# A sink as a score column, weight remainders and residual scaling on GpSimd, and first weights in pieces, in a four-layer transformer kernel

## The chip, the cores and the metric

The kernel runs on one core of one Trainium2 chip. A core has TensorE (PE) for matrix products, VectorE (DVE), ScalarE (ACT), GpSimd (POOL) and SyncE (SP), which here only issues DMAs. The engines run their own instruction streams and meet at semaphores. The metric is the device time of one launch in microseconds (us), lower is better.

## What is computed

Two blocks of two layers each, on 512 tokens of width 1024. Layers 0 and 1 hold full attention and a chunked state-space mixer. Layers 2 and 3 hold attention in a band of 128 tokens with a sink, and differential attention. The four layers end with a gated feed-forward part. The change touches the beginning and layers 2 and 3, of which this is the core:

```python
def windowed_gqa_sink(q, k, v, sink):          # 8 query heads, 2 key heads, blocks of 128
    scores = einsum(q, k) * D ** -0.5          # each block of queries sees up to 3 blocks of keys
    scores = where(|kpos - qpos| <= 128, scores, NEG)
    m = maximum(max(scores), sink)             # one number per head
    p = exp(scores - m)
    p = p / (sum(p) + exp(sink - m))
    return einsum(p, v)

def diff_attention(q, k, v, lam):              # 4 heads, two score maps each
    p = softmax(einsum(q, k) * Dk ** -0.5)
    return einsum(p[:, :, 0] - lam * p[:, :, 1], v)
```

The first block ends with `rms_norm(x, final_norm_w)`, so that the residual which enters layer 2 has to be multiplied by that weight and by the reciprocal root of its mean square ("residual scaling").

## The kernel before

**Exact products from rounded ones.** An f32 operand is split into hi (rounded by ACT, as `fp32r`) and lo (the remainder f32 - hi, formed by DVE). A product is three matmuls, hi*hi, hi*lo and lo*hi (`three`, lines 1568 to 1570, which all large products share).

**Weights.** They come in groups g of 128 x 2048 (1 MB), 190 in all, through two sets of buffers by the parity of g: `w_raw` (DMA), `w_hi` (ACT, `split_hi`, line 321), `w_lo` (DVE, `split_lo`, line 771). PE waits for `w_ready`, which w_lo raises (`enter`). SP loads group g once w_lo of g - 2 is done. `split_hi(g)` waits until PE is through with group g - 2.

**Start.** SP issues the parameters, group 0, the eight tiles of x (128 x 512), group 1, the constants. ACT makes w_hi of group 0, then for each tile h_mix_hi and its square, then w_hi of group 1. DVE makes w_lo of group 0, eight h_mix_lo (`norm_lo`, line 777), then w_lo of group 1. GpSimd sums the squares (line 1495). PE makes the projection of the two groups for four blocks of tokens t: all t over k = 0 to 3 of group 0, then over k = 4 to 7 of group 1. Within the second it sums the squares by matmuls with a column of ones (`stats`, line 1632); from it come var (DVE, line 788) and rstd (GpSimd, line 1503), by which evictions scale.

**Layers 2 and 3.** They take 9 groups of projections, counted from g0, then four of w_out. While PE is at groups g0 + 3 to g0 + 8, DVE rotates heads (`rope_b(n, t)`: n = 0 queries of the band, 1 and 2 queries and keys of the differential part, t = block), for which GpSimd raises variances to -1/2 (line 1545).

**Banded attention** has 16 steps i of a block and a head pair (i = 4t + j), software-pipelined by hand. In one round PE makes scores of step i (line 1671) and adds masks by bf16 matmuls with an identity (line 1679), turns the probabilities of step i - 2 (line 1703) and multiplies those of i - 3 with v (line 1727). DVE takes maxima of the two heads' scores (line 1373), the minimum with the negated sink (line 1377), copies half of the turned probabilities (line 905). ACT makes the exps (line 408) and the other half (line 416). Scores alternate between two pairs of PSUM banks: scores of i wait for exps of i - 2. Between the rounds PE also turns the eight tiles of the differential q and k (`turn`, line 1654) through one bank, each waiting for hi (ACT, line 400) and lo (DVE, line 888) of the tile before. Once in a block the softmax factors are made (DVE line 1391, PE line 1714), applied (line 911) and split (lines 426 and 917).

Into the same rounds, in program order, are put w_hi and w_lo of two groups of w_out (rounds 12 and 14), and in layer 2 the eight residual scalings on DVE (line 1411, rounds 7 to 14).

**Differential attention** follows with 16 steps of its own: maxima (line 1423), exps (line 730), a combination of the two maps (line 1435), transposes (line 2107), products (line 2121).

## Time and profile before

| | us |
|---|---|
| median of 3 runs | 2510.55 (2508.02 to 2511.35) |
| the profiled execution, its own time | 2512.78 |
| its span, first to last instruction | 2510.6 |
| PE busy | 2430.3 (97%) |
| DVE busy | 1474.9 (59%) |
| ACT busy | 944.8 (38%) |
| GpSimd busy | 210.5 (8%) |

The profile is one execution. Busy time of PE says little by itself, since matmuls overlap and their ends are modelled; the distance between the starts of consecutive matmuls tells more: 0.23 us for 512 columns when PE runs at its higher clock. Waits are read from the timeline, where a row carries in square brackets how long its engine had been idle before it and which instruction released it.

### The profile page before, as it was taken

The page shows a single profiled execution, that of the slowest core. Times are in us where ns is not written, and L with a number is a line of the kernel's source. Part 1 is how long each engine was busy: PE and PEld are TensorE (multiplying, and loading weights), DVE is VectorE, ACT ScalarE, POOL GpSimd, SP SyncE. Part 2 cuts the span into 40 slices and gives each one's busy share as a digit, 9 for nine tenths or more (in the row PEclk, how much of TensorE's full clock was granted, in tenths as well). Part 3 has the DMA queues.
Part 4 walks back from the last instruction along what each step waited for, and adds up shares of the span by engine and source line. Part 5 has one row for each costly group of instructions (what it writes and reads, how often), then busy time and mean ns, then how long its engine had stood idle before and what let it go on. Part 6 is the DMA issues. An engine that isn't in the chain of part 4 may idle for free.

```text
span 2510.6 us, 30919 instructions
## 1 busy us (share of the span) xinstructions
PE 2430.3 (97%) x12468; PEld 1989.0 (79%) x12468; DVE 1474.9 (59%) x2074; ACT 944.8 (38%) x1496; POOL 210.5 (8%) x143
## 2 busy tenths in 40 slices
PE   7999999999999999999999799999999989999999
PEld 6767888888876788888887578888888767888887
DVE  5867543435586754343567766545466776655554
ACT  4465322213446432222444563222243465322222
POOL 2001200000200110000132011000012101100000
PEclk9999999999999999999999899999999999999999
DMA  4200222222311032222321002222232110222222
GB/s 172 78 35 1 101 96 89 101 101 101 102 68 35 1 103 99 101 95 90 118 84 68 35 9 102 94 100 101 91 111 99 53 35 25 94 101 101 100 85 101
DMA packets 30238, 205.32 MB, mean 82 GB/s; under 512 B 3344, under 2 KB 3472, under 8 KB 6288
## 3 DMA queue, kind: packets, MB, share of 16 engines
q1 hardware_dynamic: 30096, 203.35, 22.8%
q8 instruction: 99, 1.62, 0.3%
q14 instruction: 43, 0.35, 0.0%
HBM read 201.24 MB, written 2.10 MB: 81 GB/s over the span
## 4 chain that ended last, share of the span: by engine, by line
PE 85%; DVE 8%; DVEq 3%; ACT 2%; issue 1%; ACTq 0%; DMA 0%; POOL 0%; SPq 0%
PE bank L1568 25%; PE bank L1570 25%; PE bank L1569 25%; PE bank L1727 1%; PE bank L1671 1%; PE bank L1703 1%; PE bank L1953 1%; PE bank L1901 1%; PE bank L1714 1%; PE bank L1654 1%; DVE w_lo L771 1%; DVE b_p L1435 1%; DVE neg_max L1423 1%; ACT w_hi L321 1%; DVEq L1430 1%
## 5 line engine op out<-in xcount | busy, mean ns | idle before, releaser
L771 DVE TENSOR_TENSOR w_lo<-w_raw,w_hi 128x2048 fp32r<-128x2048 f32 (+1 forms) x190 | 434.0, 2284 | 404.9 <-ACT w_hi L321 404.4
L1568 PE MATMUL bank<-h_ffn_hi,w_hi 128*128 128x512 f32 x1408 | 548.6, 390 | 0.0
L1570 PE MATMUL bank<-h_ffn_hi,w_lo 128*128 128x512 f32 x1408 | 547.8, 389 | 0.0
L1569 PE MATMUL bank<-h_ffn_lo,w_hi 128*128 128x512 f32 x1408 | 547.7, 389 | 0.0
L321 ACT ACTIVATE w_hi<-w_raw 128x2048 fp32r<-128x2048 f32 (+1 forms) x190 | 360.1, 1895 | 473.0 <-PE bank L1570 424.5
L1570 PEld LDWEIGHTS bank<-h_ffn_hi,w_lo 128*128 128x128 f32 x1408 | 264.3, 188 | 55.1
L1569 PEld LDWEIGHTS bank<-h_ffn_lo,w_hi 128*128 128x128 f32 x1408 | 264.3, 188 | 54.7
L1568 PEld LDWEIGHTS bank<-h_ffn_hi,w_hi 128*128 128x128 f32 x1408 | 264.3, 188 | 54.5
L1568 PE MATMUL bank<-act_hi,w_hi 128*128 128x512 f32 x704 | 273.9, 389 | 0.0
L1569 PE MATMUL bank<-act_lo,w_hi 128*128 128x512 f32 x704 | 273.9, 389 | 0.0
L1570 PE MATMUL bank<-act_hi,w_lo 128*128 128x512 f32 x704 | 273.9, 389 | 0.0
L1568 PE MATMUL bank<-w_hi,h_mix_hi 128*128 128x512 f32 (+2 forms) x512 | 191.0, 373 | 20.1 <-DVE h_mix_lo L777 13.5
L442 ACT ACTIVATE act_hi<-up 128x512 fp32r<-128x512 f32 x88 | 55.7, 633 | 371.0 <-DVE up L950 371.0
L1495 POOL TENSOR_TENSOR sq_sum<-sq_sum,sq 128x512 f32<-128x512 f32 x56 | 95.5, 1706 | 1180.7 <-ACT sq L339 1178.6
L1569 PE MATMUL bank<-w_lo,h_mix_hi 128*128 128x512 f32 (+2 forms) x512 | 187.8, 367 | 0.0
L1570 PE MATMUL bank<-w_hi,h_mix_lo 128*128 128x512 f32 (+2 forms) x512 | 187.7, 367 | 0.0
L947 DVE TENSOR_TENSOR up<-bank,rstd_bc 128x512 f32<-128x512 f32 x88 | 60.9, 692 | 193.9 <-PE bank L1570 193.9
L1569 PEld LDWEIGHTS bank<-act_lo,w_hi 128*128 128x128 f32 x704 | 132.1, 188 | 27.5
L1570 PEld LDWEIGHTS bank<-act_hi,w_lo 128*128 128x128 f32 x704 | 132.1, 188 | 27.5
L1568 PEld LDWEIGHTS bank<-act_hi,w_hi 128*128 128x128 f32 x704 | 132.1, 188 | 27.3
L929 DVE TENSOR_TENSOR gate<-bank,rstd_bc 128x512 f32<-128x512 f32 x88 | 60.8, 691 | 117.6 <-PE bank L1570 115.9
L1568 PEld LDWEIGHTS bank<-w_hi,h_mix_hi 128*128 128x128 f32 x512 | 97.3, 190 | 39.1 <-issue 14.3
(305 smaller groups left out, 3396.3 us busy)
## 6 DMA issues: line engine op xcount, KB each, us to landing
w_raw<-weights SPq DMA_DIRECT2D x186, 1024.0 KB, 4.7
w_raw<-weights SPq DMA_DIRECT2D x4, 544.0 KB, 3.7
residual<-x_in SPq DMA_DIRECT2D x8, 256.0 KB, 5.8
x_out<-residual SPq DMA_DIRECT2D x8, 256.0 KB, 2.0
cst<-consts SPq DMA_DIRECT2D x1, 960.0 KB, 10.2
par_b<-params_b SPq DMA_DIRECT2D x1, 627.0 KB, 11.2
par_a<-params_a SPq DMA_DIRECT2D x1, 244.0 KB, 2.7
```

The source lines that it names most:

```text
L321: nc.scalar.activation(w_hi[s][:, cols], w_raw[s][:, cols], ACT.Copy).then_inc(w_hi_done, 1)
L442: act.activation(act_hi[:, 2 * i + j, :], up[j][:, :], ACT.Identity).then_inc(act_hi_done, 1)
L771: nc.vector.tensor_tensor(w_lo[s][:, cols], w_raw[s][:, cols], w_hi[s][:, cols].bitcast(F32), ALU.subtract).then_inc(w_ready, 1)
L929: nc.vector.tensor_tensor(gate[j][:, 1:SEQ + 1], bank[src][:, :], rstd_bc[:, :], ALU.mult).then_inc(bank_free[src], 1)
L947: nc.vector.tensor_tensor(up[j][:, :], bank[src][:, :], rstd_bc[:, :], ALU.mult).then_inc(bank_free[src], 1)
L1423: nc.vector.tensor_reduce(neg_max[:, n:n + 1], bank[DS_BANKS[i % 2][c]][:, :], AX.X, ALU.max, negate=True).then_inc(dmax_done, 1)
L1430: dve.drain()
L1435: nc.vector.scalar_tensor_tensor(p1, p2, tiny[:, i:i + 1], p1, ALU.mult, ALU.add).then_inc(dw_done, 1)
L1495: nc.gpsimd.tensor_tensor(sq_sum[:, :], sq_sum[:, :], sq[k % 2][:, :], ALU.add).then_inc(sum_done, 1)
L1568: mm(out, ahi, bhi, start=start, stop=False)
L1569: mm(out, ahi, blo, start=False, stop=False)
L1570: return mm(out, alo, bhi, start=False, stop=stop)
```

## The change

1. *Sink.* TensorE writes the sink as one more column behind the scores of each head: a product of 64 rows of the sink value with one column of the identity. Maximum and exp run over that column too, so that the minimum with the negated sink, the separate exps and their sum into the denominator go. Each maximum releases its own exp.
2. *Remainders and residual in layers 2 and 3.* w_lo of groups g0 + 9 and g0 + 10 goes to GpSimd, in four pieces of 512 columns each, with the residual scaling as two products a tile. ACT makes their w_hi in halves, in rounds 4, 5, 8 and 9. DVE waits for both before it uses the residual.
3. *Start.* Groups 0 and 1 come in four pieces each, alternating with the tiles of x. PE goes through k outside and t inside.
4. *Smaller moves.* In layers 2 and 3 `split_hi(g0 + 2)` stands ahead of the wait for rstd, and `split_lo(g0 + 4)` after the second rope and not the fourth. The differential maximum runs over both banks in one instruction.

```diff
             for k in range(KT):
+                cols = first_cols(k)
+                sp.dma_start(w_raw[k // 4][:, cols], weights[k // 4][:, cols]).then_inc(first_in[k], 16)
                 sp.dma_start(residual[:, k, :], x_in[:, k, :]).then_inc(x_arrived[k], 16)
-            sp.dma_start(w_raw[1][:, :], weights[1]).then_inc(w_in[1], 16)
...
+                cols = slice(part * GW // 2, (part + 1) * GW // 2)
+                nc.scalar.activation(w_hi[s][:, cols], w_raw[s][:, cols], ACT.Copy)
+                if part == 1:
+                    act.drain().then_inc(w_hi_done, 1)
...
-            split_hi(0)
             for k in range(KT):
+                cols = first_cols(k)
+                act.wait_ge(first_in[k], 16)
+                nc.scalar.activation(w_hi[k // 4][:, cols], w_raw[k // 4][:, cols], ACT.Copy).then_inc(w_hi_done if k % 4 == 3 else first_hi, 1)
                 wait_tile(-1, 24 + k)
                 norm_hi(h_mix_hi, k, mix_weight(0, k))
-                norm_square(0, k)
-            split_hi(1)
+                if k >= 1:
+                    norm_square(0, k - 1)
+            norm_square(0, KT - 1)
...
+                split_hi(g0 + 2)
                 act.wait_ge(rstd_ready, 2 * lay + 1)
-                split_hi(g0 + 2)
...
                 for i in range(20):
-                    if i >= 4 and i % 4 == 0 and i < 17:
-                        sink_exp(i // 4 - 1)
-                    if i in (12, 14):
-                        split_hi(g0 + 3 + i // 2)
+                    if i in (4, 5, 8, 9):
+                        split_half(g0 + IN_B + i // 8, i % 2)
...
                     if i < 16:
-                        pair_exp(lay, i, 0, window(i // 4)[1] * P, probs)
+                        pair_exp(lay, i, 0, window(i // 4)[1] * P + 1, probs)
...
                 for t in range(TB):
                     rope_b(0, t)
-                split_lo(g0 + 4)
+                    if t == 1:
+                        split_lo(g0 + 4)
...
-                        nc.vector.tensor_reduce(neg_max[:, c:c + 1], bank[S_BANKS[i % 2][par_]][:, 0:window(i // 4)[1] * P],
-                                                AX.X, ALU.max, negate=True)
-                    dve.drain()
-                    j = i % 4
-                    nc.vector.tensor_tensor(neg_max[:, 2 * i:2 * i + 2], neg_max[:, 2 * i:2 * i + 2], neg_sink[:, 2 * j:2 * j + 2],
-                                            ALU.min).then_inc(max_done, 2)
+                        nc.vector.tensor_reduce(neg_max[:, c:c + 1], bank[S_BANKS[i % 2][par_]][:, 0:window(i // 4)[1] * P + 1],
+                                                AX.X, ALU.max, negate=True).then_inc(max_done, 1)
...
-                    dve.wait_ge(sink_out, 4 * l + t + 1)
                     dve.wait_ge(e_done, base + 8 * t + 8)
-                    nc.vector.tensor_tensor(denom[:, c], denom[:, c], tiny[:, c], ALU.add)
-                    dve.drain()
                     nc.vector.reciprocal(recip[:, c], denom[:, c]).then_inc(recip_ready, 1)
...
-                    if i in (12, 14):
-                        split_lo(g0 + 3 + i // 2)
-                    if l == 0 and 7 <= i < 7 + KT:
-                        k = i - 7
-                        nc.vector.scalar_tensor_tensor(residual[:, k, :], residual[:, k, :], par_a[:, 0, A_FIN + k:A_FIN + k + 1],
-                                                       rstd_bc[:, :], ALU.mult, ALU.mult)
...
-                    for c in range(2):
-                        n = 2 * i + c
-                        dve.wait_ge(ds_done, 32 * l + n + 1)
-                        nc.vector.tensor_reduce(neg_max[:, n:n + 1], bank[DS_BANKS[i % 2][c]][:, :],
-                                                AX.X, ALU.max, negate=True).then_inc(dmax_done, 1)
+                    dve.wait_ge(ds_done, 32 * l + 2 * i + 2)
+                    nc.vector.tensor_reduce(neg_max[:, 2 * i:2 * i + 2], both_banks(DS_BANKS[i % 2], 512),
+                                            AX.X, ALU.max, negate=True).then_inc(dmax_done, 2)
...
+                    for n in range(4):
+                        cols = slice(n * GW // 4, (n + 1) * GW // 4)
+                        nc.gpsimd.tensor_tensor(w_lo[s][:, cols], w_raw[s][:, cols], w_hi[s][:, cols].bitcast(F32), ALU.subtract)
+                    pool.drain().then_inc(w_ready, 1)
...
+                split_lo(g0 + IN_B)
+                if l == 0:
+                    pool.wait_ge(bc_ready, broadcasts(2 * lay) + 1)
+                    for k in range(KT):
+                        x = residual[:, k, :]
+                        nc.gpsimd.tensor_tensor(x, x, par_a[:, 0, A_FIN + k:A_FIN + k + 1].to_broadcast([P, SEQ]), ALU.mult)
+                        pool.drain()
+                        if k == 3:
+                            split_lo(g0 + IN_B + 1)
+                        nc.gpsimd.tensor_tensor(x, x, rstd_bc[:, :], ALU.mult)
+                    pool.drain().then_inc(x_scaled, 1)
+                else:
+                    split_lo(g0 + IN_B + 1)
...
+                for k in range(KT):
+                    s, kk = divmod(k, 4)
+                    if kk == 3:
+                        pe.wait_ge(w_ready, s + 1)
+                    else:
+                        pe.wait_ge(first_ready, 3 * s + kk + 1)
+                    pe.wait_ge(h_ready, k + 1)
+                    if k == KT - 1:
+                        pe.wait_ge(consts_ready, 1)
+                        stats(0)
+                    for t in range(TB):
...
                 if masked:
+                    for par_ in range(2):
+                        rows = slice(par_ * HD, (par_ + 1) * HD)
+                        head = B_SINK + 2 * j + par_
+                        mm(bank[S_BANKS[i % 2][par_]][:, nb * P:nb * P + 1], par_b[rows, lay - LAYERS, head:head + 1].to_broadcast([HD, P]),
+                           ident[rows, par_ * HD:par_ * HD + 1], start=False, stop=False)
```

**ACT at the start of the program.** Before:

```order
L321 ACT_TABLE_LOAD [waits w_in0]
L321 ACTIVATE w_hi<-w_raw 128x2048 [waits par_in]
L332 ACTIVATE h_mix_hi<-residual,par_a 128x512 [waits x_arrived0]
L339 ACTIVATE sq_sum<-residual 128x512
L332 ACTIVATE h_mix_hi<-residual,par_a 128x512 [waits x_arrived1]
```

And now:

```order
L491 ACT_TABLE_LOAD [waits first_in0]
L491 ACTIVATE w_hi<-w_raw 128x512 [waits par_in]
L350 ACTIVATE h_mix_hi<-residual,par_a 128x512 [waits x_arrived0]
L491 ACTIVATE w_hi<-w_raw 128x512 [waits first_in1]
L350 ACTIVATE h_mix_hi<-residual,par_a 128x512 [waits x_arrived1]
L357 ACTIVATE sq_sum<-residual 128x512
```

The first tile of h_mix_hi stands behind a quarter of a group and not a whole one, and a square comes one tile later.

**DVE in round 12 of the banded attention of layer 2** (the exps of the second to last block; L771 is w_lo, L1411 the residual scaling). Before:

```order
L1373 TENSOR_REDUCE neg_max<-bank 128x1 [waits s_done] x2
L1377 TENSOR_TENSOR neg_max<-neg_max,neg_sink 128x2
L888 TENSOR_TENSOR b_kt_lo<-bank,b_kt_hi 128x512 [waits t_hi_done]
L905 COPY b_pt<-bank 128x384 [waits o_done,pt_done]
L771 TENSOR_TENSOR w_lo<-w_raw,w_hi 128x2048 [waits w_hi_done]
L1411 SCALAR_TENSOR_TENSOR residual<-residual,par_a,rstd_bc 128x512
L917 TENSOR_TENSOR b_ot_lo<-b_on,b_ot_hi 128x4x128 [waits o_hi_done]
L1389 TENSOR_TENSOR denom<-denom,tiny 128x8 [waits e_done,sink_out]
L1391 RECIPROCAL recip<-denom 128x8
```

And now:

```order
L1393 TENSOR_REDUCE neg_max<-bank 128x1 [waits s_done] x2
L903 TENSOR_TENSOR b_kt_lo<-bank,b_kt_hi 128x512 [waits t_hi_done]
L920 COPY b_pt<-bank 128x384 [waits o_done,pt_done]
L932 TENSOR_TENSOR b_ot_lo<-b_on,b_ot_hi 128x4x128 [waits o_hi_done]
L1400 RECIPROCAL recip<-denom 128x8 [waits e_done]
```

The minimum, w_lo, the scaling and the sum with the sink's exp are gone from DVE's row.

**GpSimd in layer 2**, from the last powers for the ropes (head_rs) on. Before:

```order
L1549 TENSOR_TENSOR head_rs<-ssq,neg_half 128x4x2 [waits hvar_ready]
L1545 TENSOR_TENSOR head_rs<-ssq,neg_half 128x8 [waits hvar_ready] x8
L1554 TENSOR_TENSOR head_rs<-ssq,neg_half 128x4 [waits gn_var] x4
L1495 TENSOR_TENSOR sq_sum<-sq_sum,sq 128x512 [waits sq_done] x7
L1503 TENSOR_TENSOR rstd<-var,neg_half 128x4 [waits var_ready]
```

And now:

```order
L1546 TENSOR_TENSOR head_rs<-ssq,neg_half 128x8 [waits hvar_ready] x8
L1560 TENSOR_TENSOR w_lo<-w_raw,w_hi 128x512 [waits w_hi_done,w_ready]
L1560 TENSOR_TENSOR w_lo<-w_raw,w_hi 128x512 x3
L1569 TENSOR_TENSOR residual<-residual,par_a 128x512 [waits bc_ready]
L1573 TENSOR_TENSOR residual<-residual,rstd_bc 128x512
...
L1569 TENSOR_TENSOR residual<-residual,par_a 128x512
L1560 TENSOR_TENSOR w_lo<-w_raw,w_hi 128x512 [waits w_hi_done,w_ready]
L1560 TENSOR_TENSOR w_lo<-w_raw,w_hi 128x512 x3
L1573 TENSOR_TENSOR residual<-residual,rstd_bc 128x512
```

The first remainder and, behind it, the two products for each tile have come to GpSimd; the second remainder stands between the two products of tile 3.

## Rows read from the trace of the kernel before

**Rows 1.** Page part 4, shares of the chain that ended last, by engine.

```profile
PE 85%; DVE 8%; DVEq 3%; ACT 2%; issue 1%; ACTq 0%; DMA 0%; POOL 0%; SPq 0%
```

**Rows 2.** Timeline, start: start us, us, engine, line, operation, count [idle before <-releaser].

```profile
6.04 1.28 ACT L321 ACT_TABLE_LOAD   x1 [6.04 <-DMA w_raw<-weights]
...
7.33 1.91 ACT L321 ACTIVATE w_hi<-w_raw 128x2048 fp32r<-128x2048 f32 x1
...
9.35 2.29 DVE L771 TENSOR_TENSOR w_lo<-w_raw,w_hi 128x2048 fp32r<-128x2048 f32 x1 [8.35 <-ACT w_hi L321]
...
13.55 0.77 PE L1568 MATMUL bank<-w_hi,h_mix_hi 128*128 128x512 f32 x1 [13.55 <-DVE h_mix_lo L777]
```

**Rows 3.** Windows: length, PE, PEld, DVE, ACT, POOL (count), granted clock, DMA, GB/s.

```profile
13.50:19.60 6.10, 5.99 (x12) 3.41 (x13) 6.10 (x4) 4.62 (x8) 5.62 (x4) 1.00 0.81 338
19.60:33.20 13.60, 13.60 (x61) 11.25 (x60) 9.42 (x25) 2.44 (x2) 3.10 (x2) 1.00 0.12 41
1312.40:1317.00 4.60, 4.53 (x13) 3.59 (x14) 4.28 (x10) 0.00 (x0) 1.64 (x1) 0.63 0.64 228
1373.80:1433.80 60.00, 48.24 (x474) 36.72 (x474) 42.38 (x97) 34.96 (x101) 0.00 (x0) 0.89 0.10 36
1996.70:2054.20 57.50, 47.61 (x462) 36.31 (x462) 36.08 (x86) 33.78 (x97) 0.00 (x0) 0.88 0.11 38
1433.80:1480.00 46.20, 39.23 (x283) 29.75 (x281) 41.03 (x90) 35.55 (x105) 3.03 (x3) 0.96 0.00 1
```

**Rows 4.** Timeline, from stats to w_lo of the third group of layer 0.

```profile
33.45 0.94 PE L1632 MATMUL bank<-ones,sq_sum 128*128 128x1 f32 x8
...
35.73 1.11 ACT L321 ACTIVATE w_hi<-w_raw 128x1088 fp32r<-128x1088 f32 x1 [13.66 <-POOL rstd L1503]
...
36.88 1.29 DVE L771 TENSOR_TENSOR w_lo<-w_raw,w_hi 128x1088 fp32r<-128x1088 f32 x1 [2.28 <-ACT w_hi L321]
```

**Rows 5.** Timeline, PE's waits for w_lo in layers 2 and 3.

```profile
1286.55 0.39 PE L1568 MATMUL bank<-w_hi,h_mix_hi 128*128 128x256 f32 x1 [1.31 <-DVE w_lo L771]
...
1312.47 0.50 PE L1568 MATMUL bank<-w_hi,h_mix_hi 128*128 128x512 f32 x1 [2.34 <-DVE w_lo L771]
...
1935.64 0.50 PE L1568 MATMUL bank<-w_hi,h_mix_hi 128*128 128x512 f32 x1 [2.83 <-DVE w_lo L771]
```

**Rows 6.** Timeline, end of layer 0: sums of squares on GpSimd beside DVE.

```profile
617.46 2.26 POOL L1495 TENSOR_TENSOR sq_sum<-sq_sum,sq 128x512 f32<-128x512 f32 x1 [331.43 <-ACT sq L339]
...
618.49 1.79 DVE L777 SCALAR_TENSOR_TENSOR h_mix_lo<-residual,par_a,h_mix_hi 128x512 fp32r<-128x512 f32 x1
...
622.28 1.34 POOL L1495 TENSOR_TENSOR sq_sum<-sq_sum,sq 128x512 f32<-128x512 f32 x1 [2.56 <-ACT sq L339]
...
622.43 0.69 DVE L794 TENSOR_TENSOR residual<-bank,residual 128x512 f32<-128x512 f32 x1
```

**Rows 7.** Chain in order of time, rounds 5 and 6 of layer 2: start, us, what.

```profile
1387.06 1.02 PE bank L1714 x16
...
1388.52 0.72 PE bank L1671 x6
```

**Rows 8.** Groups by line and form, DVE, band of layer 2: busy us, mean ns.

```profile
L1373 DVE TENSOR_REDUCE neg_max<-bank 128x1 f32<-128x384 f32 x16 | 8.1, 549 | 4.8 <-PE bank L1679 4.8
L1411 DVE SCALAR_TENSOR_TENSOR residual<-residual,par_a,rstd_bc 128x512 f32<-128x512 f32 x8 | 5.9, 744 | 0.0
...
L771 DVE TENSOR_TENSOR w_lo<-w_raw,w_hi 128x2048 fp32r<-128x2048 f32 x2 | 4.6, 2282 | 0.0
...
L1377 DVE TENSOR_TENSOR neg_max<-neg_max,neg_sink 128x2 f32<-128x2 f32 x15 | 2.4, 160 | 1.1
```

**Rows 9.** Timeline, two waits of PE in the band of layer 2.

```profile
1412.98 0.39 PE L1671 MATMUL bank<-b_kd_hi,h_mix_hi 64*128 64x256 f32 x2 [1.52 <-DVE b_kt_lo L888]
...
1417.26 1.98 PE L1714 MATMUL bank<-cst,recip 128*64 128x128 f32 x16 [2.78 <-DVE recip L1391]
```

**Rows 10.** Groups by line and form, DVE, differential attention of layer 2.

```profile
L1423 DVE TENSOR_REDUCE neg_max<-bank 128x1 f32<-128x512 f32 x32 | 20.6, 685 | 1.2 <-PE bank L2097 0.8
```

76 lines of the change are left out of this document (47 added, 29 removed).

## The prediction

> **What bounds the kernel now.** I read the chain on the page first: PE carries 85% of it [rows 1]. So another engine matters only where PE waits for it. The second view was who PE waits for, the third the timeline and windows around those waits, whose rows stand here. The largest is 13.5 us before the first matmul [rows 2]; later ones name DVE (w_lo, b_kt_lo, recip) [rows 5, 9]. The reader should see two costs at each: the idle time, and the matmuls behind it at twice the pitch. The twelve matmuls from 13.5 on fill 6.1 us, against 61 in the next 13.6 us (0.22 each); at 1312.4 to 1317 the granted clock is 0.63, between the levels 1.2 and 2.4 GHz [rows 3].
>
> **Start.** Before, w_hi (1.91) and w_lo (2.29) of a whole group precede the first operand of PE, and PE begins at 13.55, released by the first h_mix_lo [rows 2]. Now each k brings 512 columns. A w_hi piece costs about 0.63 (an estimate from 1.91 for 2048 and 1.11 for 1088 columns [rows 2, 4]), a w_lo piece 0.69 in the same way from 2.29 and 1.29. The whole megabyte had landed by 6.04 [rows 2]; the three quarters that are no longer waited for are 0.79 MB, 2.3 us at the 338 GB/s of the next stretch [rows 3], so the first quarter lands near 3.8, with the par_a in front of it and the shorter run-up say 4.1. Then table load 1.28, w_hi to 6.05, h_mix_hi to 6.7, w_lo to 6.75, h_mix_lo to 7.5: PE starts at 7.5, not 13.55. The new order gives 12 matmuls per k, 5.2 us at the slow pitch and 2.72 at the fast. ACT needs 1.7 per k; DVE and GpSimd, which exclude each other here (below), about 2.6. PE is therefore the bound from k = 1 on. The first pair ends at 7.5 + 96 x 0.227 + 0.8 (stats) + 2.4 (slow phase, 9 to 14 matmuls at 0.2 extra) = 32.5, against 39.8 before (stats at 33.45, 0.8 for them, then 24 x 0.227, and 0.1 [rows 4]): 7.3 gained. But stats now stand 12 matmuls before that end and not 24. From the end of stats to w_lo of group 2 it takes 3.85 us (rstd, w_hi, w_lo [rows 4]); 2.72 of it is covered, so a new wait of 1.1 arises, and 0.2 behind it for banks freed later. **Start: 6.0** (4 to 7.5). The stages behind it are released by PE and move as a whole, since each begins with evictions of its banks.
>
> **Before the banded attention.** Layer 2 shows PE waiting 1.31 for w_lo of its third group (at 1286.55), and 2.34 at 1312.47 for that of the fifth [rows 5]. The second wait comes because DVE does this remainder (2.29) behind four ropes, so that it ends just when PE starts again. Moved two ropes (some 7 us) forward, it is done before PE asks. The slow phase goes too: 13 matmuls began in 4.6 us [rows 3], where the fast pitch needs 2.9. That is 4.2. The first wait should go as well, since w_hi no longer waits for rstd. But now w_lo starts right behind var, just when GpSimd's powers start. **A lock:** at 617.46 a GpSimd add beside w_lo took 2.26 and not 1.34, and the h_mix_lo behind it 1.79 and not 0.75; an add of DVE with one operand in PSUM ran undisturbed at 0.69 beside a GpSimd add [rows 6]. Two-input SBUF operations of both engines exclude each other. So rstd comes 2.2 later, evictions later, and of 1.46 only some 0.8 is gained. **Layer 2: 5.0** (3.5 to 5.8). Layer 3 has the second wait with 2.83 and no slow phase; 3.0, and 0.4 at the first: **3.4** (2.5 to 3.5) [rows 5]. The DVE work behind these places waits for evictions and splits that PE releases, so it moves with PE and nothing is lost again.
>
> **Banded attention.** Layer 2 takes 60.0 us from 1373.8, layer 3 57.5 [rows 3]. At full clock, PE's own work is 41.3, summed from pitches in the timeline: score and mask groups 0.68 (3 + 4 steps) and 1.05 (8), transposes 0.45 and 0.70 (8 each), products 0.44 and 0.80 (8 each), four factor groups 1.05, eight turns 0.6; a factor group and a score group stand as examples [rows 7]. The other 18.7 (16.2 in layer 3) are waits, 11.8 by PE's busy time, and slow phases behind them (granted clock 0.89 [rows 3]). In them stand DVE's two w_lo (2.28 each), eight residual scalings (0.74), neg_max with neg_sink (0.16 and the drain before it) [rows 8], and twice in a block an operation of that size for the sink's sum. PE's wait of 2.78 at 1417.26 ended with recip, behind w_lo and one scaling; that of 1.52 at 1412.98 ended with b_kt_lo, behind ACT's whole w_hi [rows 9].
>
> *Removed:* 4.6 + 5.9 + 16 x 0.35 + 4 x 0.4 = 17.7 us of DVE in layer 2, 11.8 in layer 3, and on ACT four small exps of 0.2. exp of the first head can also start after its own maximum, not after both and the minimum. *Added on PE:* two one-column products a step. Nothing like it stands in the band; the nearest row is stats, 0.8 for four blocks of 128 columns, each loaded for one column, 0.2 each [rows 4]. Bounds 0 (hidden in the 0.25 that PE idles before masks, which appear as "issue") and 0.4 a step; I take 0.3, so 4.6 a layer. *Moved on ACT:* w_hi in halves at steps 4, 5, 8 and 9, about 1.0 each, in front of exp. ACT is busy for 35.0 of the 60.0 us [rows 3], but its load over steps 4 to 9 becomes 19.6 us against 20.3 on PE, too near for no stalls. *GpSimd:* eight w_lo pieces and, in layer 2, sixteen products at 1.3 [rows 6]: 32 us from about 1385, done by 1420, while the weights and the residual are wanted at w_out after 1480: cover of 60 us. Uncovered they would cost 32. Queued behind them on GpSimd is only the power of the first differential block, some 20 us into that stage. Of DVE's work only three b_ot_lo, and perhaps recip, have all inputs in SBUF: up to 1.3 each, one on the path.
>
> Remaining waits: the turn chain of the first steps, which uses one bank (1.6 before, with its slow phase), ACT's halves, the tail. I take 6.6 in layer 2 and 5.6 in layer 3, a third of before: 41.3 + 4.6 + 6.6 = 52.5 and 51.5. **Band: 7.5 (3 to 12) and 6.0 (2 to 10).**
>
> The Trainium skill, "GPSIMD Engine Reference", section Engine selection, speaks against this part: elementwise work on a tile belongs on VectorE, GPSIMD being about twice as slow with two inputs. The row agrees (four pieces 5.3 against 2.29), and this sum stays as it is, since the rule prices the operation and not the place in which it is hidden.
>
> **Differential attention.** DVE carries it: 41.0 of 46.2 us [rows 3]. Its two maxima of 0.685 [rows 10] start 0.60 apart and hold 1.20 together; one over both banks should hold 1.13 (1.06 ns an element, from 549 ns for 384 and 685 for 512 [rows 8, 10]). exp of the first component starts 0.35 later, inside the 0.8 us by which de_done precedes its use. **1.0 a layer, 2.0** (-2 to 3).
>
> **Sum.** 6.0 + 5.0 + 3.4 + 7.5 + 6.0 + 2.0 = 29.9. The profiled execution took 2512.8 (span 2510.6 and 2.2 around it): 2482.9. The median of the runs shown is 2.2 below that execution, so I forecast 2481.
>
> **Rivals.**
> *Band stays latency-bound, 0.17.* ACT's halves and the sink products take the place of DVE's remainders: the band gives 4 in all and not 13.5. For it: ACT's load above; against it: steps 5 and 6 of before, with DVE unburdened, ran on PE alone from one group to the next [rows 7]. 2490.
> *All stalls of the band go, 0.06.* 14 and 11.6 and not 7.5 and 6: 2469.
> *The lock covers every operation of DVE, 0.06.* Then 32 us of GpSimd stand in DVE's way in layer 2 and its band is 12 longer than before: 2500. Against it: the undisturbed add [rows 6]. The Trainium skill ("GPSIMD Engine Reference", Key points) limits the contention to DVE operations with two SBUF inputs or in a 2-port mode; by that rule this rival falls, and the trace agrees.
> *The sink products break PE's stream, 0.03, slower.* If PE empties its pipe before and after each (0.25 as before the masks, then 0.19 load and 0.25 product, twice) a step costs 1.4 on the path, 31 steps 43 us, against 39 gained elsewhere (29.9 + 9.2 already charged): 2515. It decides from 1.3 us a step on. Against it: four such products of stats take 0.8.
> *The parts don't act (PE waits elsewhere for as long), 0.02:* 2508.
>
> **How the numbers follow.** Forecast case 0.66, 2472 to 2490 of its own. The bounds of the terms add up to 13 and 42 gained, 2497 and 2469; the range 2467 to 2497 holds forecast, first and second rival, 0.89 less their tails. 0.2% (5 us) is about what a measurement can tell from no change. Faster 0.95, same 0.02, slower 0.03.
>
> **What would show it.** First matmul at 7 to 8 us and the end of the first pair at 31 to 34, with a wait for w_lo of 1 us behind. No wait for w_lo at the fifth group of layers 2 and 3. From scores to differential attention 49 to 57 us; one-column products at 0.3 a step; GpSimd done 50 us before w_out. Wrong if PE still waits for recip or b_kt_lo by microseconds, if w_hi halves end exps' waits, if DVE's copies and maxima grow while GpSimd runs, or if the operands at the start come slower than 2.7 us per k.

## The result and the profile after

| | us |
|---|---|
| before, median of 4 runs | 2510.41 (2508.02 to 2511.35) |
| changed, median of 4 runs | 2474.26 (2471.94 to 2477.57) |
| ratio | 0.9858, 95% interval 0.9841 to 0.9875 |
| changed, the profiled execution | 2471.94, span 2470.2 |

The changed kernel takes 36 us less; 2481 had been forecast. The chain that ended last runs over TensorE for more of the span than before [rows 1]:

```profile
PE 90%; DVE 6%; ACT 1%; DVEq 1%; issue 1%; POOL 0%; ACTq 0%; DMA 0%; SPq 0%
```

To see where the time went, I took the first start of the same product in both traces and subtracted. A gain that arises between two milestones belongs to the stretch between them.

| first start of | before | changed | gained so far |
|---|---|---|---|
| first matmul | 13.55 | 7.71 | 5.8 |
| first convolution product, layer 0 | 80.7 | 74.8 | 5.9 |
| first scores of layer 0 | 122.8 | 116.9 | 5.9 |
| first scores of layer 1 | 744.2 | 737.0 | 7.2 |
| first band scores of layer 2 | 1368.7 | 1356.3 | 12.4 |
| differential attention of layer 2 | 1433.8 | 1408.7 | 25.1 |
| first band scores of layer 3 | 1990.5 | 1961.1 | 29.4 |
| differential attention of layer 3 | 2054.2 | 2013.3 | 40.9 |
| end of the span | 2510.6 | 2470.2 | 40.4 |

The first and last starts of one line (last two numbers ahead of the shapes), before and changed, show the second and part of the fourth row:

```profile
L1828 PE MATMUL bank<-cst,a_conv x32: 271/272/328, 80.7 to 722.2; 128*128 128x128 f32 x32
```

```profile
L1879 PE MATMUL bank<-cst,a_conv x32: 271/272/328, 74.8 to 715.0; 128*128 128x128 f32 x32
```

The timeline of the changed kernel at the start answers [rows 2] and [rows 4]:

```profile
4.17 1.28 ACT L491 ACT_TABLE_LOAD   x1 [4.17 <-DMA w_raw<-weights]
...
6.21 0.69 DVE L992 TENSOR_TENSOR w_lo<-w_raw,w_hi 128x512 fp32r<-128x512 f32 x1 [5.21 <-ACT w_hi L491]
...
7.71 0.77 PE L1594 MATMUL bank<-w_hi,h_mix_hi 128*128 128x512 f32 x1 [7.71 <-DVE h_mix_lo L792]
...
30.09 0.16 DVE L803 TENSOR_SCALAR var<-bank 128x4 f32<-128x4 f32 x1 [2.31 <-PE bank L1677]
...
33.88 0.39 PE L1594 MATMUL bank<-w_hi,h_mix_hi 128*128 128x272 f32 x1 [0.94 <-DVE w_lo L786]
```

The reader sees the first matmul at 7.71 (forecast 7.5), and at 33.88 the new wait behind the sums of squares, 0.94 (forecast 1.1).

In layer 2 the wait for w_lo of the fifth group is gone. At the third group this is left (timeline):

```profile
1272.82 2.29 DVE L786 TENSOR_TENSOR w_lo<-w_raw,w_hi 128x2048 fp32r<-128x2048 f32 x1
...
1272.98 3.00 POOL L1503 TENSOR_TENSOR rstd_fin<-rstd_fin,neg_half 128x4 f32<-128x4 f32 x1 [8.08 <-DVE var L801]
...
1278.49 0.35 PE L1594 MATMUL bank<-w_hi,h_mix_hi 128*128 128x256 f32 x1 [0.49 <-ACT b_squares L482]
```

GpSimd's power on 4 elements takes 3.00 us where it starts together with w_lo.

The windows of the two bands (from the first scores to differential attention) and of the two differential attentions, columns as in [rows 3]:

```profile
1356.30:1408.70 52.40, 48.12 (x559) 39.79 (x558) 30.00 (x66) 36.10 (x101) 29.01 (x24) 1.00 0.12 42
1961.10:2013.30 52.20, 48.33 (x559) 39.81 (x558) 29.76 (x66) 36.10 (x101) 9.96 (x8) 1.00 0.12 42
1408.70:1455.10 46.40, 38.45 (x290) 29.54 (x289) 40.03 (x74) 35.30 (x105) 3.03 (x3) 1.00 0.00 1
2013.30:2060.40 47.10, 39.92 (x291) 30.66 (x289) 40.07 (x74) 35.30 (x105) 3.03 (x3) 0.96 0.00 1
```

Counted in the same way the bands took 65.1 and 63.7 us before:

```profile
1368.70:1433.80 65.10, 51.90 (x495) 39.41 (x494) 43.29 (x100) 36.28 (x103) 0.00 (x0) 0.90 0.09 34
1990.50:2054.20 63.70, 52.69 (x494) 39.92 (x494) 37.92 (x92) 36.18 (x103) 0.00 (x0) 0.89 0.10 34
```

Two columns matter: in layer 2 DVE's busy time fell from 43.29 to 30.00, and the granted clock rose from 0.90 to 1.00. The clock was not an object of the change. It fell again, to 0.90 and 0.94, in the experiment below that brings the waits of both parts back. The gain in the bands was undersized in the forecast (13.5; here 24.2), so the experiments ask which of its two parts brought what.

### The profile page after: what moved, and what is told of

It reads as the page before. It is cut to its first block, busy times and chain, and to the rows that moved or that the text cites. A ratio compares the mean times of both kernels' runs of the same rounds, so it can differ in the third digit from the quotient of the medians.

```text
span 2470.2 us, 31138 instructions
## 1 busy us (share of the span) xinstructions
PE 2416.9 (98%) x12596; PEld 1987.6 (80%) x12596; DVE 1450.5 (59%) x1986; ACT 944.9 (38%) x1498; POOL 253.0 (10%) x175
## 4 chain that ended last, share of the span: by engine, by line
PE 90%; DVE 6%; ACT 1%; DVEq 1%; issue 1%; POOL 0%; ACTq 0%; DMA 0%; SPq 0%
PE bank L1594 26%; PE bank L1595 26%; PE bank L1596 26%; PE bank L1716 1%; PE bank L1777 1%; PE bank L1753 1%; PE bank L1699 1%; DVE neg_max L1421 1%; PE bank L2004 1%; PE bank L1952 1%; PE bank L1764 1%; DVE b_p L1433 1%; PE bank L2172 0%; DVE a_conv L1041 0%; PE bank L1986 0%
## 5 line engine op out<-in xcount | busy, mean ns | idle before, releaser
L786 DVE TENSOR_TENSOR w_lo<-w_raw,w_hi 128x2048 fp32r<-128x2048 f32 (+1 forms) x184 | 420.3, 2284 | 396.0 <-ACT w_hi L329 395.4
L329 ACT ACTIVATE w_hi<-w_raw 128x2048 fp32r<-128x2048 f32 (+1 forms) x184 | 348.6, 1895 | 451.0 <-PE bank L1596 423.7
L944 DVE TENSOR_TENSOR gate<-bank,rstd_bc 128x512 f32<-128x512 f32 x88 | 60.8, 691 | 118.0 <-PE bank L1596 116.2
```

Of the source, the lines that this page charges most:

```text
L329: nc.scalar.activation(w_hi[s][:, cols], w_raw[s][:, cols], ACT.Copy).then_inc(w_hi_done, 1)
L786: nc.vector.tensor_tensor(w_lo[s][:, cols], w_raw[s][:, cols], w_hi[s][:, cols].bitcast(F32), ALU.subtract).then_inc(w_ready, 1)
L944: nc.vector.tensor_tensor(gate[j][:, 1:SEQ + 1], bank[src][:, :], rstd_bc[:, :], ALU.mult).then_inc(bank_free[src], 1)
```

## The experiments

Bands are given as lengths from the first scores to differential attention, layer 2 and layer 3, each from one profile. How far one such length can be trusted is the subject of the first experiment. Times are set against 2474.26 of the changed kernel. The runs of three later sessions were made on other chips, each beside the kernel before (2508.5 to 2509.1 there), so such a difference is uncertain by 1 to 2 us: by the ratios the first loss below, 9.6 us, would be 10 to 11.

**The changed kernel once more.**

> The changed kernel as it is, beside the three others on the same chip. Tells what of a difference is chance: in the profiles so far the full attention of layers 0 and 1, whose instructions no run changes, took 52.5 to 55.3 us. 2474 again within 2 us; if its stretches differ by that much from its first profile, the 1.3 us that the start gained beyond its own stretch was chance.

Measured: 2475.27 us (2472.82 to 2477.07), ratio 0.9862 (0.9847 to 0.9877). Windows of this run: the attention of layer 1, then the two bands.

```profile
736.60:789.10 52.50, 47.95 (x469) 36.09 (x470) 38.78 (x65) 37.45 (x89) 2.04 (x2) 1.00 0.12 42
1353.10:1408.50 55.40, 50.94 (x559) 41.87 (x558) 31.80 (x66) 36.21 (x101) 29.10 (x24) 0.94 0.11 40
1961.80:2015.10 53.30, 49.79 (x558) 40.96 (x557) 29.75 (x66) 36.10 (x101) 9.96 (x8) 0.97 0.11 41
```

In the first profile of the same kernel the attention of layer 1 was the long one:

```profile
737.00:792.30 55.30, 50.75 (x469) 38.28 (x470) 38.81 (x65) 37.50 (x89) 2.04 (x2) 0.94 0.12 39
```

In the attention of layer 1 the same instructions ran both times, with the same waits ahead of them; the difference of 2.8 us lies in the granted clock, 1.00 against 0.94. In the band of layer 2, 3.0 us longer, it is only a part. In the first profile, scores after a wait of 1.45 us ran at the full pace. In this one, the same wait of 1.45 us was followed by matmuls at half the pace from about 1360 on (four products of 128 columns in 1.12 us and not 0.66):

```profile
1358.31 0.39 PE L1716 MATMUL bank<-b_kd_hi,h_mix_hi 64*128 64x256 f32 x2 [1.45 <-ACT b_vb L478]
...
1362.19 1.12 PE L1699 MATMUL bank<-cst,b_qb 128*128 128x128 f32 x4 [0.49 <-DVE h_mix_lo L903]
```

So a wait of this size may or may not be followed by such a phase. The other part is DVE meeting GpSimd (start, us, engine, operation as before):

```profile
1382.88 1.29 POOL L1573 TENSOR_TENSOR residual<-residual,rstd_bc 128x512 f32<-128x512 f32 x1
...
1382.90 1.81 DVE L932 TENSOR_TENSOR b_ot_lo<-b_on,b_ot_hi 128x512 fp32r<-128x512 f32 x1
...
1384.89 1.09 PE L1764 MATMUL bank<-cst,recip 128*64 128x128 f32 x16 [0.41 <-DVE recip L1400]
```

Here b_ot_lo took 1.81 us and, a block later, 1.74; alone it takes 0.68. The recip behind it came late, and TensorE waited 0.41 and 0.61 for it. In the first profile the two took 0.68 and 0.91, and there is no wait for recip.

The band of layer 2, unchanged in its code and order, had 52.4 to 55.4 us in the six profiles in which it ran (this kernel twice, and four of the kernels below), that of layer 3 52.1 to 53.3. The six fall into three groups: 52.4 at full clock without the waits for recip (the first profile alone), 53.5 or 53.6 at full clock with them (two), 55.4 with them and a granted clock of 0.94 (three). So of the 3 us about 1.1 belongs to this meeting, which five of the six profiles show, and 1.9 to the clock. The 1.3 us gained between the first scores of layer 0 and those of layer 1 are chance too: this run had them as well, but others with the same code in layer 0 did not (its scores spanned 52.5 or 54.1).

**Remainders and residual back on DVE, the sink column kept.**

```diff
-                    if i in (4, 5, 8, 9):
-                        split_half(g0 + IN_B + i // 8, i % 2)
+                    if i in (12, 14):
+                        split_hi(g0 + 3 + i // 2)
...
+                    if i in (12, 14):
+                        split_lo(g0 + 3 + i // 2)
+                    if l == 0 and 7 <= i < 7 + KT:
+                        k = i - 7
+                        nc.vector.scalar_tensor_tensor(residual[:, k, :], residual[:, k, :], par_a[:, 0, A_FIN + k:A_FIN + k + 1],
+                                                       rstd_bc[:, :], ALU.mult, ALU.mult)
```

GpSimd's part and DVE's two waits for it are out as well.

> The changed kernel (2474.3 us) with one part undone: w_lo of the two groups of w_out and, in layer 2, the residual scaling are back on DVE in rounds 7 to 14, w_hi whole in rounds 12 and 14, GpSimd idle in the band. The sink column stays. The band of layers 2 and 3 gained 12.7 and 11.5 us where 7.5 and 6 were forecast. Theory A (DVE's long operations in its row caused most stalls and the slow phases behind them): layer 2's band is 6 to 9 us longer than in the changed kernel, layer 3's 3 to 6, 2484 to 2489 in all. Rival B (the latency from maximum to exp, which the sink column cuts, caused them): 2 us longer in all, 2476.

Measured: 2483.83 us, ratio 0.9902 (0.9887 to 0.9917), 9.6 us above the changed kernel; bands 60.0 and 56.7. TensorE's waits in the last third of layer 2's band:

```profile
1396.51 0.39 PE L1704 MATMUL bank<-b_kd_hi,h_mix_hi 64*128 64x256 f32 x2 [1.10 <-DVE b_kt_lo L903]
...
1400.55 1.98 PE L1752 MATMUL bank<-cst,recip 128*64 128x128 f32 x16 [2.42 <-DVE recip L1400]
...
1409.96 0.66 PE L1765 MATMUL bank<-b_pt,b_va 128*64 128x128 f32 x8 [1.26 <-DVE b_on L926]
```

These are the waits of [rows 9], at the same products and by the same releasers, 1.52 and 2.78 there. The 2.42 is followed by sixteen factor products in 1.98 us and not 1.09. The second and third end behind w_lo and a scaling (2.28 and 0.75 us) in DVE's row. The first does not: DVE itself idled there for b_kt_hi, which stood behind ACT's whole w_hi of 1.92 us, and this edit had moved that back too:

```profile
1395.77 0.69 DVE L903 TENSOR_TENSOR b_kt_lo<-bank,b_kt_hi 128x512 fp32r<-128x512 f32 x1 [1.08 <-ACT b_kt_hi L418]
```

So theory A holds for the larger waits, and 1.1 of the 4.8 us is ACT's.

**The old sink path, remainders and residual kept on GpSimd.**

```diff
-                                                AX.X, ALU.max, negate=True).then_inc(max_done, 1)
+                                                AX.X, ALU.max, negate=True)
+                    dve.drain()
+                    nc.vector.tensor_tensor(neg_max[:, 2 * i:2 * i + 2], neg_max[:, 2 * i:2 * i + 2], neg_sink[:, 2 * j:2 * j + 2],
+                                            ALU.min).then_inc(max_done, 2)
...
+                    nc.vector.tensor_tensor(denom[:, c], denom[:, c], tiny[:, c], ALU.add)
```

The sink products on TensorE are out, and the sum with the sink's exp is back on DVE and ACT.

> The changed kernel with the other part of the band undone: the sink by minimum with neg_sink, separate exps and a sum into the denominator; no sink column on TensorE. Remainders and residual stay on GpSimd. Theory A: DVE has slack once its long operations are gone, so 0.35 us a step on DVE costs little, and TensorE is spared the sink products (0.13 us a step by the distance of score and factor groups before and after, 4 us in both layers): between 2 faster and 4 slower, 2472 to 2478. Rival B: the stalls come back, 15 us slower, 2489.

Measured: 2483.78 us, ratio 0.9901 (0.9887 to 0.9916); bands 59.4 and 55.4. Neither expectation was met: I had said at most 4 us, and it was 9.5. The group of the minimum in layer 2's band, and one of its instances beside GpSimd:

```profile
L1406 DVE TENSOR_TENSOR neg_max<-neg_max,neg_sink 128x2 f32<-128x2 f32 x16 | 7.2, 451 | 1.2
```

```profile
1380.95 1.26 POOL L1596 TENSOR_TENSOR residual<-residual,rstd_bc 128x512 f32<-128x512 f32 x1
1381.13 1.10 DVE L1406 TENSOR_TENSOR neg_max<-neg_max,neg_sink 128x2 f32<-128x2 f32 x1
1382.17 1.04 POOL L1592 TENSOR_TENSOR residual<-residual,par_a 128x512 f32<-128x512 f32 x1
1382.27 0.58 ACT L428 ACTIVATE b_p<-bank,neg_max 128x384 f32<-128x384 f32 x1 [1.75 <-DVE neg_max L1406]
1382.33 0.91 DVE L1411 TENSOR_TENSOR tiny<-par_b,neg_max 128x8 f32<-128x8 f32 x1
...
1383.98 0.63 PE L1722 MATMUL bank<-cst,b_kb 128*128 128x128 f32 x4 [2.41 <-DVE h_mix_lo L911]
```

The minimum of two numbers took 1.10 us and ended as GpSimd's product did; behind it stood exp, the sink's sum (0.91, alone 0.17) and the h_mix_lo for which TensorE waited 2.41. Before, without GpSimd at work, its mean was 0.160 [rows 8].

**The old sink path with GpSimd idle** tells this lock from latency.

```diff
-                        nc.gpsimd.tensor_tensor(w_lo[s][:, cols], w_raw[s][:, cols], w_hi[s][:, cols].bitcast(F32), ALU.subtract)
...
-                        nc.gpsimd.tensor_tensor(x, x, par_a[:, 0, A_FIN + k:A_FIN + k + 1].to_broadcast([P, SEQ]), ALU.mult)
...
-                        nc.gpsimd.tensor_tensor(x, x, rstd_bc[:, :], ALU.mult)
```

> As e2_old_sink (old sink path, no sink column), and GpSimd's work in the band is left out altogether: neither the remainders of the two groups of w_out in layers 2 and 3 nor the residual scaling of layer 2 are computed, only their semaphores are raised. Tells apart why the old sink path cost 7.0 us in layer 2 and 3.2 in layer 3. Theory L (lock): its small DVE operations (128x2, 0.16 us alone, 0.45 in the mean and up to 1.10 beside GpSimd in layer 2) wait for GpSimd; with GpSimd idle they are 0.16 again and layer 2 falls from 59.4 to layer 3's 55 or below, layer 3 to 54: 2477 to 2479. Rival (latency): the longer way from maximum to exp costs TensorE as much whatever GpSimd does: 59 and 55 stay, 2483.

Measured: 2475.84 us, ratio 0.9869 (0.9855 to 0.9884); bands 54.8 and 53.6. The minimum is short again:

```profile
L1406 DVE TENSOR_TENSOR neg_max<-neg_max,neg_sink 128x2 f32<-128x2 f32 x16 | 2.6, 161 | 1.2
```

The lock, and not the latency, made the old path dear beside GpSimd: 4.6 us in layer 2 at the same granted clock of 0.97, and 1.8 in layer 3, where the clock differs too (0.97 with GpSimd at work, 1.00 without), so that part of the 1.8 may be the clock's. By the medians it is 7.9 of the 9.5. With neither engine loaded the sink column is worth little: these bands are 54.8 and 53.6, and the changed kernel's are 52.4 or 55.4 and 52.2 or 53.3. Beside GpSimd its use is that it takes from DVE's path operations that have all inputs in SBUF. What it is worth where DVE itself is loaded, the next experiment shows. The Trainium skill ("GPSIMD Engine Reference", Key points) says that GpSimd contends with DVE's instructions that have two SBUF inputs or run in a 2-port mode; the trace agrees, down to an operation of two elements, and the maxima and copies from PSUM beside it kept their 0.55.

**Both parts of the band undone.**

> The changed kernel with both parts of the band undone (sink path and GpSimd's work as before); start, the smaller moves and the merged differential maximum stay. What is left of the gain is start 7.3, the stretches before the band 5.9 and 3.4 less what is noise: 2494 to 2499 by the two traces. If the losses of the two single undoings add up to this one's, the two parts act on different stalls; if they add up to less, each part alone leaves the band bound by what the other removes; if to more, either part removes the same stalls.

Measured: 2491.69 us, ratio 0.9936 (0.992 to 0.9953), 17.4 us above the changed kernel; bands 65.4 and 60.6. This is less than the first two profiles said (24.2), for two reasons: this run's band of layer 3 has a granted clock of 0.94 and 60.6 us where that of before has 0.89 and 63.7, and the first profile of the changed kernel was its fastest run. Against the second one the two bands lose 17.3.

```profile
1353.30:1418.70 65.40, 52.18 (x493) 39.86 (x492) 43.28 (x100) 36.13 (x103) 0.00 (x0) 0.90 0.10 33
1971.10:2031.70 60.60, 49.14 (x492) 37.20 (x492) 37.85 (x92) 36.23 (x103) 0.00 (x0) 0.94 0.10 36
```

The single undoings cost 9.6 and 9.5, together 19: within the uncertainty they add up. That does not make the two parts independent, as all five medians beside each other show:

| work for w_out and residual scaling in the band | sink by minimum and exp | sink column |
|---|---|---|
| on DVE | 2491.69 | 2483.83 |
| on GpSimd | 2483.78 | 2474.26 |
| not computed | 2475.84 | not run |

Down the column of the minimum: without this work on DVE the old sink path is 15.9 us faster, and where GpSimd does it, 7.9 of them are lost again to the lock. Across: the sink column is worth 9.5 us beside GpSimd, but also 7.9 where DVE does the work and GpSimd is idle, so without any lock. (In the first row ACT's w_hi is whole and in rounds 12 and 14 as well, in the other two in halves and earlier.) In the first row TensorE's listed waits in layer 2's band add up to 13.2 us with the minimum and 8.9 with the column (4.3 less of the band's 5.4). So the column removes stalls in either case, those behind a long row of DVE or those behind GpSimd; only where neither stands in the way is little left (2475.84 against 2474.26). Which of the minimum, its drain and the shorter way to exp counts in the loaded row was not tried apart. The sums come out equal because an overlap of the two parts, the same stalls removed by either, and the lock, which the column avoids, happen to be of about one size (6.4 us, which is 15.9 and 7.9 less 17.4, and 7.9).

**Four times the sink products.**

> The changed kernel with the two sink products of each step made four times instead of once, the three extra pairs into columns that nobody reads. Prices the product: the forecast took 0.3 us a pair; starts in the trace of the changed kernel say 0.20 a pair, of which 0.07 falls into the gap that stood before the masks. Theory A (it is on TensorE's path at 0.20): 3 x 0.20 x 32 = 19 us longer, 2493. Theory B (0.3, the forecast's price): 29 us, 2503. Theory C (it hides in stalls of TensorE): under 8 us, below 2482.

Measured: 2496.53 us, ratio 0.9951 (0.9936 to 0.9966): 22.3 us for 96 more pairs, 0.23 each, between theories A and B. In the timeline the three extra pairs (twelve records) take 0.74 us:

```profile
1391.91 0.28 PE L1724 MATMUL bank<-cst,par_b 64*128 64x1 f32 x4
1392.05 0.81 PE L1730 MATMUL bank<-cst,par_b 64*128 64x1 f32 x12
1392.79 0.40 PE L1735 MATMUL bank<-mask_bf,id_bf 128*128 128x128 bf16 x4
```

The first pair costs less than that. Before, 0.27 us passed from the last score products to the masks, and in the changed kernel 0.38 with the sink products between them, starts 0.18 and 0.20 apart. Before, then changed:

```profile
1388.89 0.34 PE L1671 MATMUL bank<-b_kd_hi,h_mix_lo 64*128 64x384 f32 x2
1389.16 0.40 PE L1679 MATMUL bank<-mask_bf,id_bf 128*128 128x128 bf16 x4
```

```profile
1387.90 0.34 PE L1716 MATMUL bank<-b_kd_hi,h_mix_lo 64*128 64x384 f32 x2
1388.08 0.28 PE L1724 MATMUL bank<-cst,par_b 64*128 64x1 f32 x4
1388.28 0.40 PE L1729 MATMUL bank<-mask_bf,id_bf 128*128 128x128 bf16 x4
```

So the net price is 0.11 a step by this one step, 1.7 us a layer.

**w_hi whole and not in halves** (rounds 4 and 8).

> The changed kernel with w_hi of the two groups made whole (2048 columns, 1.9 us) in rounds 4 and 8, not in halves in rounds 4, 5, 8, 9. Theory H (the halves matter: a whole one delays the exps of its round by 1 us more, and TensorE has no slack of that size): 1 to 2 us a layer, 2476 to 2478. Rival (ACT has slack enough in these rounds): within 0.5 us, 2474.

Measured: 2472.84 us, ratio 0.9862 (0.9847 to 0.9877): no difference in time. In the trace two waits of TensorE arise in each layer, 0.76 for b_kt_lo and 0.2 for recip, bands 53.3 and 53.1. The halves are worth about 1 us a layer as waits, which these measurements can't confirm as time.

**GpSimd's remainders in one piece of 2048 columns.**

```diff
-                    for n in range(4):
-                        cols = slice(n * GW // 4, (n + 1) * GW // 4)
+                    for n in range(1):
+                        cols = slice(0, GW)
```

> The changed kernel with GpSimd's remainders in one instruction of 2048 columns (about 5 us) and not four of 512. The old sink path showed that DVE's operations with two inputs in SBUF wait for the GpSimd instruction under way. Theory S (short pieces matter even with the sink column, since b_ot_lo or recip wait up to 5 us): 2 to 4 us longer, 2477. Rival (in these stretches DVE has no such operation left, b_ot_lo stands at other times): within 0.5 us in the bands, 2474.

Measured: 2472.8 us, ratio 0.9853 (0.9838 to 0.9868), bands 54.5 and 52.2; one piece takes 4.56 us, the four took 4.97. Theory S falls. In the bands of this profile DVE has no operation of the locked kind while the remainders run; b_ot_lo, the one left, meets the residual products instead (1.39 and 1.33 us in layer 2). Whether the piece length matters on the old sink path wasn't tried.

**The two small moves undone.**

> The changed kernel with the two small moves of layers 2 and 3 undone: w_hi of group g0 + 2 again behind the wait for rstd, w_lo of group g0 + 4 again behind the fourth rope. Forecast 5.0 and 3.4 for them, trace 5.1 and 3.4: 8.5 us longer, 2483, with waits of TensorE for w_lo of 1.3 and 2.3 in layer 2 and of 2.8 in layer 3, and in layer 2 GpSimd's first power back from 3.00 to 1.02 us. Rival (a wait later in the stretch absorbs a part, since DVE's ropes end at their own pace): 4 us, 2478.

Measured: 2481.43 us, ratio 0.989 (0.9876 to 0.9905), 7.2 us above. TensorE's waits are back:

```profile
1279.03 0.39 PE L1593 MATMUL bank<-w_hi,h_mix_hi 128*128 128x256 f32 x1 [1.31 <-DVE w_lo L786]
```

```profile
1304.98 0.80 PE L1593 MATMUL bank<-w_hi,h_mix_hi 128*128 128x512 f32 x1 [2.39 <-DVE w_lo L786]
```

and 2.46 in layer 3. GpSimd's first power is back at 1.02. From the last scores of layer 1 to the first of layer 2 it takes 569.1 us again and not 564.0: the forecast's 5.0 is 5.1. The stretch from the first product with w_out of layer 2 to the first scores of layer 3 is 3.1 longer (in the kernel before, 3.7 longer). By the median 7.2 of the expected 8.5 came, nearer to the forecast than to the rival's 4.

**Differential maxima apart.**

> The changed kernel with the differential maxima of the two components apart again. Forecast was 2.0 us gained by merging them; the traces show 0.2 a layer at equal clock. Theory P: the steady step is 0.06 shorter merged (2.33 against 2.39), 0.9 a layer, and the prologue is 0.6 longer (the first exp starts after both maxima: TensorE's two waits for it are 2.2 each, before 1.6): 0.3 a layer, 2474 to 2475, with the waits at 1.6. Rival (the merge gained its 1.0 a layer and slow clock phases hid it): 2476 to 2477.

Measured: 2473.07 us, ratio 0.9861 (0.9845 to 0.9877): no difference. At the head of the stage the exps' wait is 1.57 and that for b_p 1.17; merged they are 2.21 and 0.50, nearly the same sum, so the prologue was not where the gain went, as theory P had it:

```profile
1411.75 0.50 PE L2150 MATMUL bank<-b_kt_hi,h_mix_hi 64*128 64x512 f32 x2 [1.57 <-ACT b_p L745]
...
1413.88 0.66 PE L2160 MATMUL bank<-cst,b_p 128*128 128x128 f32 x4 [1.17 <-DVE b_p L1435]
```

```profile
1412.55 0.50 PE L2148 MATMUL bank<-b_kt_hi,h_mix_hi 64*128 64x512 f32 x2 [2.21 <-ACT b_p L745]
...
1414.01 0.66 PE L2158 MATMUL bank<-cst,b_p 128*128 128x128 f32 x4 [0.50 <-DVE b_p L1433]
```

The group of the merged maxima in layer 2 holds 19.5 us and not 20.6 [rows 10], but DVE idles 1.3 us in front of them, for TensorE's scores. Layer 3 of the kernel before, also at full clock, had 0.5 there (second row):

```profile
L1421 DVE TENSOR_REDUCE neg_max<-bank 128x2 f32<-128x1024 f32 x16 | 19.5, 1222 | 1.3 <-PE bank L2148 1.3
```

```profile
L1423 DVE TENSOR_REDUCE neg_max<-bank 128x1 f32<-128x512 f32 x32 | 20.6, 684 | 0.5
```

At full clock the stage's scores spanned 38.5 to 38.8 us merged and 38.7 to 38.8 apart. In five further stretches with merged maxima at full clock the idle time is 1.3 each, and 0.5 in the one other with them apart. So most of the 1.1 us that DVE's busy time lost is idle time now, and little of it is gained in the stage.

**The old order of products with the new pieces.**

```diff
-                for k in range(KT):
+                for s in range(2):
+                    for t in range(TB):
+                        for kk in range(4):
```

> The changed kernel with the pieces of the first weights kept, but TensorE in the old order: within a group all k of one block of tokens, then the next block, and the sums of squares 24 and not 12 matmuls before the end of the pair. Tells what of the start's 5.9 us is due to the pieces and what to the order. By the pace of operands in the trace of the changed kernel (about 2 us per k) TensorE gets 12 matmuls in the first 7 us, then has to catch up: the pair ends near 34.7 and not 32.9, the wait of 0.9 behind it goes: 1 to 3 us longer, 2476. Rival (the order brings nothing, since the end is set by matmuls after the operands are there): 1 us shorter.

Measured: 2475.57 us, ratio 0.9865 (0.9848 to 0.9881), by time no different from the changed kernel on the same chip (2475.27). In the trace TensorE starts at 7.65 and then waits 0.29 and 1.74 for operands; group 2 begins at 36.90 where the changed kernel begins it at 33.88, and the first scores of layer 0 at 119.8, in the eleven profiles of the other kernels with the new order, the next experiment apart, at 116.2 to 117.3. Of the start's 5.9 us the order of products carries about 3 (2.0 of them in the two waits), at the upper end of what was expected, and the pieces the rest; since the median doesn't show the 3 us, this rests on the traces.

```profile
14.57 0.77 PE L1594 MATMUL bank<-w_hi,h_mix_hi 128*128 128x512 f32 x1 [1.74 <-DVE h_mix_lo L792]
```

**An addition: group g0 + 2 ahead of the sums of squares.** The diff shows DVE; in layers 0 and 1 ACT's w_hi moves in the same way, and the first differential maximum is taken for each component apart.

```diff
+                split_lo(g0 + 2)
                 norm_stats(2 * lay)
-                split_lo(g0 + 2)
```

> The changed kernel with three small additions from the traces: w_hi and w_lo of group g0 + 2 are made ahead of the sums of squares in all four layers (ACT before its wait for rstd, DVE before var), so that DVE's w_lo no longer locks out GpSimd's powers and TensorE finds it ready; and the first of the 16 differential maxima is taken for each component apart. Expected from the waits: 0.9 at the start, 0.5 in layer 2, 0 to 0.4 in layers 1 and 3, 0.6 in each differential attention: 2.5 us less, 2471.8; GpSimd's first power of layer 2 at 1.02 and not 3.00 us. Rival: other waits (evictions of the first pair behind rstd) come in at once, under 1 us in all.

Measured: 2472.95 us (2471.82 to 2473.45), ratio 0.9853 (0.9838 to 0.9868), on the same chip as 2475.27 for the changed kernel. It is 1.4% faster than the kernel before; against the changed kernel the 2.3 us agree with the expected 2.5, but the intervals overlap, and the kernel with the remainders in one piece, of which no gain was expected, showed as much on that chip. So that it beats the changed kernel is supported by the trace and not shown by the times. In the trace the waits of 0.94 and 0.49 are gone, the differential's waits for exp add up to 3.1 and not 4.4 (those for b_p to 11.7 and not 10.7, so most of it comes back), and the power has no w_lo beside it:

```profile
1270.79 1.13 POOL L1509 TENSOR_TENSOR rstd_fin<-rstd_fin,neg_half 128x4 f32<-128x4 f32 x1 [8.11 <-DVE var L801]
```

## Why the prediction was right, point by point

| term | forecast | measured |
|---|---|---|
| start | 6.0 (4 to 7.5) | 5.9 by the trace |
| before the band, layer 2 | 5.0 | 5.1 |
| before the band, layer 3 | 3.4 | 3.1 (moves undone) to 3.7 (before and changed) |
| band, layers 2 and 3 | 7.5 and 6.0 | 12.7 and 11.5 in the first profile, 9.7 and 10.4 in the second; 17.4 together by the medians |
| differential attention | 2.0 | 0, within the measurement |

The range held, and the sum came within 7 us, partly because two errors of opposite sign met: the bands gave 4 to 11 us more than forecast, the differential attention 2 less.

- *Start.* First matmul 7.71 for 7.5, the new wait 0.94 for 1.1. The step that worked was to follow one operand through table load, w_hi, w_lo and h_mix_lo, and then to ask whether TensorE's own pace in its slow phase is longer than the next operand's. That phase is read from the starts (0.43 us apart for 512 columns until 12.5, then 0.23); the column of the granted clock says 1.00 there, as it does in the first window of [rows 3], and doesn't show it.
- *Before the bands.* Both moves did what was forecast, the lock of GpSimd's power by w_lo included (3.00 us for 1.02, so 2.0 later and not 2.2). The 4.2 written for the fifth group of layer 2 is 4.0 by its own terms (2.34 and 4.6 less 2.9), with no effect on the sum that could be measured.
- *Bands.* The forecast was short here, and two terms were mis-sized. The sink pair was taken at 0.3 a step; its net price is 0.11, 2.9 us less in a layer. The stalls left were taken at a third of the old ones, 6.6 and 5.6; in the first profile, at full clock, TensorE's listed waits after the second scores add up to 2.5 (0.96, 0.36, 0.57, 0.23 and 0.40). The sum of the two, 7.0, is more than the 5.2 by which the band of layer 2 beat the forecast, so my 41.3 for TensorE's own work was some 2 us too low. The step that was off was to scale waits and the slow phases behind them together by one factor. The phases can vanish: the granted clock went from 0.90 to 1.00 in one profile, and to 0.94 in the next.
- *GpSimd.* It finished at 1403.6, for 1420 forecast, and the weights were wanted after 1455: a cover of 51 us, where the text said 60 and the signs 50. Not seen beforehand was that the two parts of the band depend on each other: without the sink column GpSimd's work would have cost some 6 to 8 us through the lock. The prediction named the lock, but weighed it only against what the changed kernel still has on DVE. There it was about right: up to 1.3 us for each b_ot_lo had been said, up to 1.13 was measured, and TensorE waited 0.4 and 0.6 for the recip behind it in five of six profiles.
- *Differential attention.* Here a saving on the busiest engine was taken for one of the stage. DVE was 41.0 of 46.2 us busy, yet a step's maxima also wait for TensorE's scores. The later exp was not hidden at the head of the stage either, where TensorE's wait for it grew from 1.6 to 2.2. The merged maximum itself took 1.22 us; by the slope in the text (1.06 ns an element from 685 ns for 512) it is 1.23, and 1.13 only if the 0.08 by which two in a row overlapped before is taken off.
- *Rivals.* The nearest was that all stalls of the band go (2469, given 0.06). The measured 2474.3 is closer to it than to the forecast of 2481, and the first profile's 12.7 and 11.5 are close to its 14 and 11.6. It did not come as written, since waits of 2.5 us stayed in the band and the medians give the two parts 17.4 and not 25.6. The others are refuted. That of the latency (2490) is refuted by TensorE's waits in the band of the changed kernel, that of the lock on every operation (2500) by maxima and copies of 0.55 us beside GpSimd, that of the broken stream (2515) by 0.23 a pair.

What stays open: why a wait of the same length is followed by a slow phase in one execution and not in another, and with it how much of the 17 to 24 us of the two bands belongs to the change. The Trainium skill ("TensorE: Matmul & The Clock Gate", Part 1) says that the same kernel shows more or fewer slow matmuls at its start from run to run. The traces agree: in the two profiles of the changed kernel the first 11 and the first 9 matmuls are followed only after 0.4 us or more by the next. Here the same holds in the middle of a kernel too.

## What to carry to other kernels

Before work is moved to GpSimd, list what DVE still has to do meanwhile with all inputs in SBUF: even a minimum of two numbers a partition waits until the GpSimd instruction under way ends, and everything queued behind it too. Moving that small work elsewhere (here a column that TensorE writes) is what makes the GpSimd part nearly free. When two parts of a change are undone one by one and the losses add up, look at the remaining corners before calling them independent: here an overlap and a conflict cancelled. Where the first matmul waits for a chain over a whole buffer, cut the buffer by the contraction index and put that index outside, and when waits are removed from a TensorE stage, count the slow matmuls behind them as a term of its own with bounds from nothing to all.
